# A convolution, attention and expert trunk on one core: the depthwise stage cut by token tile, and TensorE's block of it as banded steps

## The reference

```python
def conformer_conv_module(h, norm_g, pw1_w, pw1_b, dw_w, dw_b, ln_g, ln_b, pw2_w, pw2_b):
    hn = rms_norm(h, norm_g)
    a, gate = jnp.split(hn @ pw1_w + pw1_b, 2, axis=-1)
    u = a * jax.nn.sigmoid(gate)
    u = lax.conv_general_dilated(u, dw_w[:, None, :], window_strides=(1,), padding=[(CONV_WIDTH - 1, 0)],
        dimension_numbers=('NWC', 'WIO', 'NWC'), feature_group_count=D_MODEL) + dw_b     # 31 taps, depthwise
    u = jax.nn.silu(layer_norm(u, ln_g, ln_b))
    return u @ pw2_w + pw2_b

h = h + conformer_conv_module(h, ...)
h = h + hierarchical_moe(h, ...)      # top 2 of 8 experts in the best of 4 groups; weights 6 MB an expert
```

## Time and profile before

| | before |
|---|---|
| median of 3 runs | 1112.23 us (lowest 1110.93) |
| span of the profiled execution | 1109.2 us |
| TensorE busy | 990.5 us, 89% |
| VectorE busy | 239.2 us, 22% |
| ScalarE busy | 172.5 us, 16% |
| GpSimd busy | 58.4 us, 5% |
| DMA queue of SyncE | 429.86 MB, 95% of 16 engines' span |
| mean granted TensorE clock | 0.988 |

### The profile page before, as it was taken

How to read it: one execution, slowest core, us unless ns; L and a number is a source line. 1 busy time by engine, 2 the same in 40 slices (tenths; PEclk the granted TensorE clock), 3 DMA queues, 4 the chain that set the end, 5 groups by cost and what they waited for, 6 DMA issues and landing times.

```text
span 1109.2 us, 11451 instructions
## 1 busy us (share of the span) xinstructions
PE 990.5 (89%) x4832; PEld 431.6 (39%) x4832; DVE 239.2 (22%) x530; ACT 172.5 (16%) x435; POOL 58.4 (5%) x92
## 2 busy tenths in 40 slices
PE   8999999989798979879799999998897989798886
PEld 7885533223232323223255654332323232232332
DVE  6993420101020100101026624101010101020101
ACT  3865300000000000000044513000000000000000
POOL 2990000000000000000000000000000000000000
PEclk9999999999999999999999999999999999999999
DMA  9795999999999999999997669999999999999997
GB/s 316 216 362 209 333 430 426 427 428 427 428 428 425 429 428 426 429 429 425 400 381 236 210 211 390 428 429 425 428 430 426 427 431 427 426 428 429 427 422 300
DMA packets 67215, 430.73 MB, mean 388 GB/s; under 512 B 12262, under 2 KB 22589, under 8 KB 46428
## 3 DMA queue, kind: packets, MB, share of 16 engines
q1 hardware_dynamic: 67038, 429.86, 95.0%
q10 hardware_dynamic: 126, 0.14, 0.0%
HBM read 428.94 MB, written 1.05 MB: 388 GB/s over the span
## 4 chain that ended last, share of the span: by engine, by line
DMA 48%; PE 38%; DVE 7%; SPq 5%; issue 1%; ACT 1%; DVEq 0%
DMA ring<-in_w_down_dram 21%; DMA ring<-in_w_gate_up_dram 21%; PE bank L964 12%; PE bank L1013 6%; DVE bank L1369 4%; SPq L459 4%; DMA zone<-in_w_down_dram 4%; PE bank L953 3%; PE bank L1062 3%; PE bank L1265 3%; PE bank L902 2%; DMA zone<-in_w_gate_up_dram 2%; PE bank L1152 1%; PE bank L1174 1%; PE bank L1128 1%; PE bank L1022 1%
## 5 line engine op out<-in xcount | busy, mean ns | idle before, releaser
L964 PE MATMUL bank<-ring,zone 128*32 128x512 f32 x1152 | 325.5, 605 | 47.6 <-DMA ring<-in_w_gate_up_dram 30.9
L964 PE MATMUL bank<-zone 128*32 128x512 f32 x872 | 263.8, 606 | 31.7 <-DMA zone<-in_w_gate_up_dram 16.0
L964 PEld LDWEIGHTS bank<-ring,zone 128*32 128x32 f32 x1152 | 85.6, 111 | 224.0 <-issue 223.5
L1013 PE MATMUL bank<-ring,xT 128*32 128x512 f32 x496 | 141.6, 599 | 11.9 <-DMA ring<-in_w_down_dram 8.6
L964 PEld LDWEIGHTS bank<-zone 128*32 128x32 f32 x872 | 67.7, 111 | 146.9 <-issue 146.8
L1492 DVE TENSOR_TENSOR xT<-xT,bank 128x512 f32<-128x512 f32 x16 | 11.0, 687 | 465.6 <-PE bank L964 465.6
L1497 DVE TENSOR_TENSOR h<-bank,h 128x512 f32<-128x512 f32 x64 | 44.2, 691 | 256.4 <-PE bank L1062 256.4
L1013 PE MATMUL bank<-zone,xT 128*32 128x512 f32 x272 | 91.6, 593 | 4.4 <-DMA ring<-in_w_down_dram 2.0
L700 ACT ACTIVATE xT<-bank 128x512 f32<-128x512 f32 x16 | 9.6, 597 | 546.1 <-PE bank L964 546.1
L1013 PEld LDWEIGHTS bank<-ring,xT 128*32 128x32 f32 x496 | 37.6, 111 | 83.2 <-issue 77.9
L953 PEld LDWEIGHTS bank<-zone,xn 128*128 128x128 f32 x512 | 58.6, 192 | 14.5 <-issue 14.5
(11 more groups left out here) (266 smaller groups left out, 668.3 us busy)
## 6 DMA issues: line engine op xcount, KB each, us to landing
ring<-in_w_gate_up_dram SPq DMA_DIRECT2D x72, 2048.0 KB, 36.8
zone<-in_w_gate_up_dram SPq DMA_DIRECT2D x54, 2048.0 KB, 35.5
ring<-in_w_down_dram SPq DMA_DIRECT2D x40, 2048.0 KB, 36.1
zone<-in_w_down_dram SPq DMA_DIRECT2D x20, 2048.0 KB, 36.8
ring<-in_a_pw_w_dram SPq DMA_DIRECT2D x8, 1024.0 KB, 12.1
ring<-in_w_down_dram SPq DMA_DIRECT2D x8, 1024.0 KB, 17.7
ring<-in_a_pw_w_dram SPq DMA_DIRECT2D x2, 2048.0 KB, 11.1
ring<-in_w_o_dram SPq DMA_DIRECT2D x2, 2048.0 KB, 20.9
```

Source lines behind the costliest of these rows:

```text
L964: ins = nc.tensor.matmul(bank[b][s * CAP:(s + 1) * CAP, :], xs[:, k, s * CAP:(s + 1) * CAP], rhs[s][:, b * HALF:(b + 1) * HALF], start=(k ...
L1013: ins = nc.tensor.matmul(bank[2 + b][s * CAP:(s + 1) * CAP, :], hidT[:, k, s * CAP:(s + 1) * CAP], units[s][:, k, b * HALF:(b + 1) * HALF] ...
```

## The change

- **TensorE's block 6.** Instead of 31 matmuls with diagonals, 16 steps on each half of the rows (64 channels). A step's weights (`banded`, 64 rows by 128) hold two diagonals: one for tap s and one for tap s + 16. The output of a half has its early taps on its own 64 partitions and its later taps on the other 64, shifted by 16 tokens, so 15 of the 16 steps are 272 columns wide. ScalarE copies the later taps down (`later_taps`), VectorE adds both and the bias. VectorE makes all the banded weights in one product of the folded identity and the taps, ahead of the angles; ScalarE's diagonals go.
- **Blocks 5 and 7 by tile.** VectorE does blocks 0, 2, 3 as before, then block 5 and its part of block 7 (now 24 taps) for tile 0 on 128 tokens, and later the same for tile 1 (31 and 16 taps). Between the taps of tile 1 stand block 6's sum, the mean's subtraction and the scaling of tile 0. ScalarE's and GpSimd's parts of block 7 follow (7 and 15 products of 128 tokens).
- **Norm and second product by tile.** Mean and variance of tile 0 stand ahead of the second product. Those of tile 1 stand inside its first two parts, after 5 and after 3 matmuls.
- **Start.** inv_freq and positions are loaded after the first weights of the first product instead of after the bias row. The first product's first half block is made tile by tile, and the transposes of the depthwise weights come behind it. Unit 5 now takes slot 8 and unit 6 slot 6, which waits for the second mean.

```diff
-        diag = spot(2 * UNIT, CW, P)
+        HALVES = (0, P // 2)
+        STEPS = (CW + 1) // 2
+        WIDE = S + STEPS
+        banded = spot(2 * UNIT, STEPS, P)
+        band_taps = spot(2 * UNIT + STEPS * P, STEPS, 2)
+        eye2 = spot(2 * UNIT + STEPS * P + 2 * STEPS, P // 2)
+        later_taps = spot(2 * UNIT + STEPS * P + 2 * STEPS + P // 2, S)
...
-        ON_DVE, ON_POOL, ON_PE, SHARED, SPLIT = (0, 2, 3, 5), (1, 4), 6, 7, 16
+        ON_DVE, ON_POOL, ON_PE, BY_TILE, SHARED, SPLIT = (0, 2, 3), (1, 4), 6, 5, 7, (24, 16)
         PRODUCTS = 10
-
-        SUMS = [(ON_POOL[0], cv[:, ON_POOL[0], :], side[0], 0), (ON_POOL[1], cv[:, ON_POOL[1], :], side[1], 0), (SHARED, side[2], side[3], SPLIT)]
+        MEAN_AT, VAR_AT = 5, 3
+        TAPS_A, TAPS_B, TAPS_C = 8, 5, 12
+
+        SUMS = [(ON_POOL[0], cv[:, ON_POOL[0], :], side[0], 0, 0, S), (ON_POOL[1], cv[:, ON_POOL[1], :], side[1], 0, 0, S),
+                (SHARED, side[2][:, 0:P], side[3][:, 0:P], SPLIT[0], 0, P), (SHARED, side[2][:, P:S], side[3][:, P:S], SPLIT[1], P, P)]
...
-        slot_order = ((9, 0, 1, 2, 3, 6, 8, 4, 5, 7), (5, 4, 3, 2, 8, 9, 6, 7, 0, 1))
+        slot_order = ((9, 0, 1, 2, 3, 8, 6, 4, 5, 7), (5, 4, 3, 2, 8, 9, 6, 7, 0, 1))
...
+            sp.dma_start(inv_freq[:, :], a["inv_freq"].to_broadcast([P, HR])).then_inc(pos_in, 16)
+            sp.dma_start(pos_i[:, :], a["positions"][0].rearrange("(t p) -> p t", p=P), allow_slow_non_contiguous=True).then_inc(pos_in, 16)
             pw1_in(1)
             sp.dma_start(pw2_b_row, a["a_pw2_b"].to_broadcast([P, D])).then_inc(small_in, 16)
-            sp.dma_start(inv_freq[:, :], a["inv_freq"].to_broadcast([P, HR])).then_inc(pos_in, 16)
-            sp.dma_start(pos_i[:, :], a["positions"][0].rearrange("(t p) -> p t", p=P), allow_slow_non_contiguous=True).then_inc(pos_in, 16)
...
+                if g == 6:
+                    sp.wait_ge(mean_done, 2)
                     sp.wait_ge(ang_ready, 1)
...
-                for _ in range((8, 0, 6, 6, 6, 6, 0, 0)[m]):
-                    if (i := next(diags, None)) is not None:
-                        nc.scalar.activation(diag[:, i, :], ident[:, :], ACT.Copy, scale=dwT[:, ON_PE, i:i + 1]).then_inc(diag_ready, 1)
-            act.wait_ge(pe_conv_done, 1)
-            nc.scalar.activation(cv[:, ON_PE, :], bank[2][:, 0:S], ACT.Identity, bias=col("dw_b", ON_PE)).then_inc(conv_act, 1)
-
-            for t in range(TT):
+
+            for i, r in enumerate(HALVES):
+                act.wait_ge(pe_conv_done, 1)
+                nc.scalar.copy(later_taps[r:r + P // 2, :], bank[4 + i][P // 2 - r:P - r, STEPS:STEPS + S]).then_inc(conv_act, 1)
+            for p in made:
+                product(p)
+
+            def squares(t):
...
-            pe.wait_ge(dw_in, 32)
-            for m in range(KD):
-                ins = nc.tensor.transpose(bank[6][:, m * CW:(m + 1) * CW], dw_rows[0:CW, m * P:(m + 1) * P], ident[0:CW, 0:CW])
-            ins.then_inc(cols_tr, 1)
-            pe.wait_ge(xT_ready, 3)
-            pe.wait_ge(xT_act, 1)
...
+                    for t, w in ((0, P), (1, P)) if m + part == 0 else ((0, S),):
+                        if m + part == 0:
+                            pe.wait_ge(xT_ready, 1 + 2 * t)
+                            pe.wait_ge(xT_act, 1)
+                        for k in range(KD):
+                            ins = nc.tensor.matmul(bank[4 + m % 4][:, part * S + t * P:part * S + t * P + w],
+                                                   pw1_sb[2 * (m // 2) + part][:, k, (m % 2) * P:(m % 2 + 1) * P],
+                                                   xT[:, k, t * P:t * P + w], start=(k == 0), stop=(k == KD - 1))
+                    if m + part == 0:
+                        pe.wait_ge(dw_in, 32)
+                        for j in range(KD):
+                            tr = nc.tensor.transpose(bank[6][:, j * CW:(j + 1) * CW], dw_rows[0:CW, j * P:(j + 1) * P], ident[0:CW, 0:CW])
+                        tr.then_inc(cols_tr, 1)
...
-            for w in range(CW):
-                pe.wait_ge(diag_ready, w + 1)
-                ins = nc.tensor.matmul(bank[2][:, 0:S], diag[:, w, :], u_sb[:, ON_PE, w:w + S], start=(w == 0), stop=(w == CW - 1))
+            pe.wait_ge(band_ready, 1)
+            for step in (0, STEPS - 1) + tuple(range(1, STEPS - 1)):
+                n = WIDE if step < STEPS - 1 else S
+                for i, r in enumerate(HALVES):
+                    ins = nc.tensor.matmul(bank[4 + i][:, 0:n], banded[r:r + P // 2, step, :], u_sb[r:r + P // 2, ON_PE, step:step + n],
+                                           start=(step == 0), stop=(step == STEPS - 2))
             ins.then_inc(pe_conv_done, 1)
...
+            mean(0)
+            variance(0)
...
-            pw2(0, 0)
-            pw2(0, 1)
+            pw2(0, 0, range(0, MEAN_AT))
+            mean(1)
+            pw2(0, 0, range(MEAN_AT, KD))
+            pw2(0, 1, range(0, VAR_AT))
+            variance(1)
+            pw2(0, 1, range(VAR_AT, KD))
...
+            V.tensor_tensor(eye2, ident[:, 0:P // 2], ident[:, P // 2:P], ALU.add)
+            link(V.memset(band_taps, 0.0))
+            for i, r in enumerate(HALVES):
+                V.tensor_copy(band_taps[r:r + P // 2, :, i], dwT[r:r + P // 2, ON_PE, 0:STEPS])
+                ins = V.tensor_copy(band_taps[r:r + P // 2, 0:CW - STEPS, 1 - i], dwT[r:r + P // 2, ON_PE, STEPS:CW])
+            link(ins)
+            V.tensor_tensor(banded.rearrange("p s (j c) -> p s j c", j=2), eye2.unsqueeze(1).unsqueeze(1).to_broadcast([P, STEPS, 2, P // 2]),
+                            band_taps.unsqueeze(3).to_broadcast([P, STEPS, 2, P // 2]), ALU.mult).then_inc(band_ready, 1)
...
+            for n, m in enumerate(ON_DVE):
+                finish(tapped(n, m, CW, 0, S))
+            finish(tapped(3, BY_TILE, CW, 0, P))
+            finish(tapped(4, SHARED, SPLIT[0], 0, P))
+            dve.wait_ge(cols_tr, 3)
+            V.tensor_copy(cols[:, N_EARLY:N_ROWS], bank[3][:, 0:N_ROWS - N_EARLY]).then_inc(cols_ready, 1)
...
+            job = tapped(5, BY_TILE, CW, P, P)
+            some(job, TAPS_A)
+            for i, r in enumerate(HALVES):
+                dve.wait_ge(conv_act, i + 1)
+                ins = V.scalar_tensor_tensor(out=cv[r:r + P // 2, ON_PE, :], in0=bank[4 + i][r:r + P // 2, 0:S],
+                                             scalar=col("dw_b", ON_PE)[r:r + P // 2, :], in1=later_taps[r:r + P // 2, :],
+                                             op0=ALU.add, op1=ALU.add)
+            ins.then_inc(conv_dve, 1)
+            some(job, TAPS_B)
+            centred(0)
+            some(job, TAPS_C)
+            scaled(0)
+            finish(job)
+            finish(tapped(6, SHARED, SPLIT[1], P, P))
+            centred(1)
+            scaled(1)
```

119 lines of the change are left out of this document (61 added, 58 removed).

## The result

| | before | after |
|---|---|---|
| median | 1111.58 us (1110.85 at the lowest) | 1120.7 us (1119.62 to 1121.93) |
| span of the profiled execution | 1109.2 us | 1118.8 us |
| TensorE, VectorE, ScalarE, GpSimd busy | 990.5, 239.2, 172.5, 58.4 us | 1001.3, 250.8, 165.7, 57.2 us |
| mean granted TensorE clock | 0.988 | 0.974 |

The ratio is 1.0085 with a 95% interval of 1.0071 to 1.0099: slower by 9 us, within 2%. Four executions of each ran on one chip. The forecast was 1122 (1115 to 1127), and 1118.8 for the span. One of the four executions of the kernel before took 5280.49 us, for a reason that no trace shows; it counts in the median of 1111.58, and the ratio leaves it out.

A forecast was written before the change was run, and what follows sets the result against it. The prediction took the second product's end, a serial head not hidden by the weight stream, as the bound. Start 3.7, second product 4.2 and clock 1.7 gave + 9.6 us: 1118.8 in the profile, 1122 us median, range 1115 to 1127.

The forecast's parts named there:

- The bound: Head of the kernel: the second product's end, 117.9 us before, sets the whole time; the weight stream does not hide it.
- M: The end of the third block on VectorE, 61.45 us in the timeline before; later times are counted from it.
- The start: Up to M: VectorE's small steps wait on GpSimd's adds, first gated block at 24.6 us, + 3.7 us.
- rival (a): Start: GpSimd does not hold VectorE up, or its adds fall elsewhere; + 0.5 instead of 3.7, 1118.6 us; chance 0.20.
- Tile 0: From M to the second product: narrow taps 0.255 us each, product start at M + 27.1, only 0.75 us earlier.
- The second product: Inside it: tile 1's mean and variance, 2 us each, and 0.95 us idle move its end by + 4.2 against M.
- The clock: Ahead of the second product: TensorE's granted clock falls to half, + 1.7 us, or 0 if it holds.
- (b): Ahead of the second product: TensorE's clock holds; 1120.1 us; chance 0.12.
- (c): Behind the second product: the weight stream hides the shift, not slower, 1112 us; chance 0.09 with its variant.
- its variant: VectorE's narrow taps at 0.195 us: product starts 4.8 us earlier, + 2.1 left, some 1114 to 1116; within (c)'s 0.09.
- (d): Second product: clock stays at half through all of it, + 27.8 us, 1147; chance 0.02.
- (e): Start: adds block in full, 5.2 us, 1123.3; with the depthwise block at half clock besides, 1126.7; chance 0.12.

The follow-up runs named there:

- Run 5: Changed kernel with mean and variance of tile 1 computed twice on TensorE, output the same: 1125.12 us, ratio to before 1.0125.
- Run 1: Changed kernel with GpSimd's two adds of the bias row to h issued behind its tap sums: 1117.81 us, ratio to before 1.0053.
- run 3: Changed kernel with eleven unneeded filler matmuls that keep TensorE busy ahead of the second product: 1118.90 us, ratio to before 1.0063.
- runs 9 and 10: Kernel before with inv_freq and positions loaded earlier, ratio 0.9993; the same with one tap of block 7 moved from GpSimd to VectorE, 0.9996.
- run 11: Kernel before with early fetch, angles ahead of the tap table's copy, and GpSimd's adds behind its sums: 1113.82 us, ratio 1.0025.
- run 12: As run 11, with GpSimd's adds waiting for VectorE's last sum and one tap of block 7 moved to VectorE: 1111.86 us, ratio 0.9994.
- run 8: Changed kernel with angles ahead of the tap table, GpSimd's adds behind its sums, and eleven filler matmuls: 1115.37 us, ratio to before 1.0029.
- runs 6 and 7: Changed kernel with norm and second product no longer by tile, 1125.54 us; the same with blocks 5 and 7 at whole width too, 1117.84 us.

## Why the prediction was right

**The bound.** Right, and the base of the rest: the second product's end moved by 9.6 us, the weight issue behind it by 9.8, the span by 9.6. Run 5 moved that end by another 4.7 us and the span by 4.7.

**The sum.** The span was met to the tenth, and that is partly luck. In pieces the forecast was 3.7 up to M, 0.6 from M to the product's start and 5.3 inside it; measured were 3.2, 1.2 and 5.3. The start was too dear by 0.5 and VectorE's chain for tile 0 too cheap by 0.6. The median was forecast 1.3 us too high for another reason: the prediction set it 3.0 us above the span, by comparing the span of one execution with the median of three, the highest of which was 5280.49 us. The four executions of the kernel after each took 1.7 to 1.8 us more than their own span, which would have given 1120.6.

**The start: + 3.7, measured + 3.2.** The place and the mechanism were right: small steps of VectorE held to the end of GpSimd's adds, then 2.3 and 2.4 us of work. The first gated block came at 24.10 instead of 24.6. The 0.5 us are in small things behind the adds' end: the copies up to the product took 0.5 instead of 0.6, the product 2.2 to the next start instead of 2.3, the angle steps 2.2 instead of 2.4; and the prediction's own terms (19.2 + 0.6 + 2.3 + 2.4) add up to 24.5. Run 1 shows what I only argued: without the adds it is 20.73. My "0.5 us later if nothing interferes" was then too high by 0.7. What rival (a) describes is run 1: 1117.81 in the median, where (a) had 1118.6.

**Tile 0.** Narrow taps 0.255, measured 5.25 / 20 = 0.26. The banded block took 7.58 us, neither my 9.5 nor 14.7: one instruction 0.118 us, where whole-array ones took 0.219. The two row halves overlap almost fully, which the neighbour row of the attention, 0.14, only hinted at. It changed nothing in the sum, as the block was costed at nothing; it made the idle stretch longer. The product started at 93.67; with M now at 64.65 that is M + 29.0, predicted M + 28.45. The missing 0.6 us are in VectorE's chain (ready for the root at M + 25.4, not 24.8), 0.2 of them in the addition of the halves, which took 1.0 and not 0.8; the other 0.4 are spread over the chain.

**The second product: + 4.2.** "2 us for the mean and 2 us for the variance" were 1.78 each, since the start of the next instruction comes 0.17 before the listed end. The idle 0.95 did not appear, because the slow first parts covered it, as the prediction allowed; with the clock held it is 0.83 (run 3).

**The clock: + 1.7.** Right: variance 3.78 us instead of 1.95, VectorE idle for 1.23 before the reciprocal (predicted 1.3), the first ten instructions 1.7 us longer (6.23 against 4.53). Run 3 takes it out and gains 1.8. The prediction miscounted the light work: it wrote 24 small matmuls and some 3 us, and there are 8 for the mean and 8 for the variance, 32 instructions or 3.8 us at full clock. The argument does not hang on it. What the prediction did not name is why TensorE stood idle at 75 to 81 us: the mean waits for VectorE's copy of the late columns at L1443 (5.90 us). By itself this wait cost nothing, since the slow mean still ended at 85.09, before VectorE came to subtract it at 85.69. But it put TensorE's light work at the end of the stretch. Whether the clock would have held with that copy earlier, no run shows.

From the product's start to its end the two errors cancel: predicted + 5.3 us, measured 33.84 - 28.58 = + 5.26.

**The rivals.** (b), the clock holds, is run 3, with 1118.90 as a median; the prediction gave it 1120.1. (c) is refuted by run 5, and its variant by the narrow tap, 0.26 us and not 0.195. (d) did not occur: the clock was 1.00 again from 98 us. (e) did not either: the start lost 3.2 us, not 5.2, and the depthwise block ran at full clock.

**What I had not seen.** The prediction treats a later start of VectorE as a plain loss, and so it was. It does not say that an earlier one would have brought next to nothing: before, VectorE's own taps, GpSimd's and TensorE's end within 1.3 us of each other (81.88, 81.60 and 80.56 us; runs 9 and 10). A change that relieves one of three such even engines and loads another loses there. This one takes 6 us from TensorE's block and 31 steps from ScalarE, and gives VectorE the table, the adding up and 7.7 us more of taps.

## What to carry to other kernels

Ask of each transferred piece of work which engine it lands on: here TensorE and ScalarE got lighter, and VectorE, whose chain sets the end, got the new steps but for two copies. Before pulling the start of one engine forward, read on all others when they end the same stage; a gain passes only as far as the next one. Before splitting a serial norm by tile, set both sides against each other: here the order by tile saved 4.8 us at the product's end, with 3.6 us of tile 1's matmuls inside the product already paid, but it needs the half-width taps, which, with the eight extra taps, cost 7.9.

## What the hardware showed that I had not expected

- Matmuls on 64 rows, alternating between the two row halves, cost 0.118 us an instruction at 272 columns (64 in 7.58 us), where whole-array ones of 256 columns took 0.219. The Trainium skill, "TensorE: Matmul & The Clock Gate", Part 3, has matmuls on different row groups run concurrently; the trace agrees, and here it is nearly a factor of two.
- Whether GpSimd's add held a step of VectorE went, in these traces, by that step's operands, and not by its size. Held: a copy of 64x16 from SBUF to SBUF (2.33 us, alone 0.17), a sum with both inputs in SBUF (2.47, alone 0.43). Not held: a memset (0.09), a difference with one input in PSUM (1.29, the same as without). The same two adds cost 3.4 us in one place, 2 and more in a second, and nothing in a third (runs 1, 11, 12).
- The granted clock at one place can differ between executions of the same instructions: at 10 to 12 us it is 0.50 in run 12 and 1.00 in run 11, whose start is written the same. Run 8 has 0.50 there too. How busy TensorE was just ahead does not tell them apart: in 8 to 10 us it was busy 1.73 us of 2 in run 12 and 1.64 in run 8, but only 1.57 and 1.26 in runs 6 and 7, which kept 1.00. In run 12 it put the first gated block off by 2.0 us against run 11. A difference of 2 us between two single profiles of this kernel therefore proves little without the windows beside it.
